# A two-layer model in fp32: feed-forward layers with one single chunk and five pairs of seven products, T3 summed by VectorE

## The reference

```python
D_MODEL = 1024
D_FF = int(math.ceil(8 * D_MODEL / 3 / 256) * 256)      # 2816

def swiglu(x, w_gate, w_up, w_down):
    return (jax.nn.silu(x @ w_gate) * (x @ w_up)) @ w_down

for i in range(DEPTH):                                  # DEPTH = 2
    ...
    u = rms_norm(h, ffn_norm_g[i])
    h = h + swiglu(u, ffn_w_gate[i], ffn_w_up[i], ffn_w_down[i])
    gate = jax.nn.sigmoid(rms_norm(h, ple_norm_g[i]) @ ple_w_gate[i])
    h = h + gate * (p[i] @ ple_w_proj[i])
```

## Time and profile before

| what | value |
|---|---|
| median of 3 runs (lowest to highest) | 1003.75 us (1002.15 to 1005.62) |
| the profiled execution: time | 1003.63 us |
| the profiled execution: span | 1001.6 us |
| PE, TensorE matmul, busy | 988.1 us, 99% |
| DVE, VectorE, busy | 775.3 us, 77% |
| ACT, ScalarE, busy | 609.2 us, 61% |
| POOL, GpSimd, busy | 153.6 us, 15% |
| DMA | 242.01 MB, 242 GB/s on average |

### The profile page before, as it was taken

The page is one execution under the profiler, slowest core; times in us unless marked ns, Lnnn a source line. Parts: engine busy times, 40 slices in busy tenths (PEclk is TensorE's granted clock), DMA queues, the critical chain, the costliest instruction groups (busy, mean ns, idle before and its releaser), DMA issues.

```text
span 1001.6 us, 13597 instructions
## 1 busy us (share of the span) xinstructions
PE 988.1 (99%) x5350; PEld 835.5 (83%) x5350; DVE 775.3 (77%) x909; ACT 609.2 (61%) x722; POOL 153.6 (15%) x150
## 2 busy tenths in 40 slices
PE   8999999999999999999999999999999999999997
PEld 8977888888778888788888888788888889999886
DVE  6996888879567666787988857876877788777874
ACT  6437567657376668666676646754857574444733
POOL 4992101101030320111111002100100010000000
PEclk9999999999999999999999999999999999999999
DMA  8862899999784632779999864577789898545631
GB/s 324 256 217 90 274 298 324 334 300 305 209 292 161 238 128 85 256 264 300 331 343 338 256 218 167 189 256 280 262 258 341 237 311 299 186 169 179 220 126 43
DMA packets 37726, 242.01 MB, mean 242 GB/s; under 512 B 4504, under 2 KB 7064, under 8 KB 9760
## 3 DMA queue, kind: packets, MB, share of 16 engines
q1 hardware_dynamic: 23904, 167.26, 43.8%
q0 software_dynamic: 10736, 70.71, 28.2%
q10 hardware_dynamic: 3024, 3.18, 1.3%
HBM read 237.91 MB, written 3.21 MB: 241 GB/s over the span
## 4 chain that ended last, share of the span: by engine, by line
PE 80%; DVE 8%; DMA 6%; issue 3%; ACT 1%; POOL 0%; SPq 0%; ACTq 0%; POOLq 0%; DVEq 0%
PE bank L441 45%; PE bank L564 18%; DVE bank L2160 4%; PE bank L427 4%; PE bank L429 4%; PE bank L428 4%; DMA raw<-in_ws 4%; DMA arena<-in_ws 3%; PE bank L478 2%; DVE w_lo L1857 2%; PE bank L603 1%; PE bank L847 0%; DMA u_scr<-arena 0%; PE bank L944 0%; PE bank L977 0%
## 5 line engine op out<-in xcount | busy, mean ns | idle before, releaser
L1857 DVE TENSOR_TENSOR w_lo<-raw,w_hi 128x2048 fp32r<-128x2048 f32 x145 | 332.8, 2303 | 84.0 <-ACT w_hi L1297 83.7
L1297 ACT ACTIVATE w_hi<-raw 128x2048 fp32r<-128x2048 f32 x156 | 298.2, 1912 | 107.9 <-PE bank L441 71.3
L1297 ACT ACTIVATE w_hi<-arena 128x2048 fp32r<-128x2048 f32 x48 | 92.4, 1924 | 57.2 <-PE bank L441 21.0
L441 PE MATMUL bank<-w_hi,x_hi 128*128 128x512 f32 x416 | 115.0, 398 | 0.2
L1857 DVE TENSOR_TENSOR w_lo<-arena,w_hi 128x2048 fp32r<-128x2048 f32 x48 | 109.2, 2285 | 5.3 <-ACT w_hi L1297 5.2
L441 PE MATMUL bank<-w_lo,x_hi 128*128 128x512 f32 x416 | 111.5, 390 | 0.0
L441 PE MATMUL bank<-w_hi,x_lo 128*128 128x512 f32 x416 | 111.5, 390 | 0.0
L441 PE MATMUL bank<-w_hi,z_hi 128*128 128x512 f32 x320 | 94.2, 394 | 0.3 <-DVE z_lo L1972 0.3
L441 PE MATMUL bank<-w_lo,z_hi 128*128 128x512 f32 x320 | 92.9, 390 | 0.1
L441 PE MATMUL bank<-w_hi,z_lo 128*128 128x512 f32 x320 | 92.9, 390 | 0.0
L441 PEld LDWEIGHTS bank<-w_hi,x_lo 128*128 128x128 f32 x416 | 78.1, 188 | 16.8
(11 more groups left out here) (292 smaller groups left out, 1592.3 us busy)
## 6 DMA issues: line engine op xcount, KB each, us to landing
raw<-in_ws SPq DMA_DIRECT2D x156, 1024.0 KB, 7.3
arena<-in_ws POOLq DMA_DIRECT2D x60, 1024.0 KB, 11.4
arena<-u_scr ACTq DMA_DIRECT2D x16, 142.0 KB, 4.9
arena<-in_rows POOLq DMA_DIRECT2D x2, 1024.0 KB, 6.6
toep<-bias_row POOLq DMA_DIRECT2D x1, 1536.0 KB, 44.7
h<-in_x_tok SPq DMA_DIRECT2D x2, 512.0 KB, 4.0
raw<-in_ws SPq DMA_DIRECT2D x2, 512.0 KB, 8.0
arena<-in_rows POOLq DMA_DIRECT2D x2, 512.0 KB, 7.5
```

What stands on the lines that cost most here:

```text
L441: ins = pe.matmul(dst, tok(a_part, k, t), w_part[:, s, c], start=first and j == 0 and i == 0, stop=last and j == 2 and i == len(ks) - 1)
L1297: act.activation(w_hi[:, g % SPLIT, :], operand(g), ACT.Copy).then_inc(hi_done, 1)
L1857: dve.tensor_tensor(w_lo[:, g % SPLIT, :], operand(g), w_hi[:, g % SPLIT, :].bitcast(F32), ALU.subtract).then_inc(lo_done, 1)
```

## The change

Chunk 0 stays single. The pairs are now (1,2), (3,4), (5,6), (7,8) and (9,10), so each layer has five pairs instead of four and one single chunk instead of three. Within the first and the last pair there is one down, within the others two, and the downs 7, 10 and 9 come last. B21's product p2 now stands second in a pair, behind B11's. T3's accumulating DMA on GpSimd's queue is gone: VectorE adds B21 to T2 in place, behind T2's low part, and SyncE's reload of B21's slot waits for that. The banks of a pair alternate between (2, 1, 0) and (1, 2, 0) for (b1, b4, b2). The first T2 is summed behind chunk 0's last quarter.

```diff
-STEPS = (0, 1, (2, 3), (4, 5), (6, 7), (8, 9), 10)
+STEPS = (0, (1, 2), (3, 4), (5, 6), (7, 8), (9, 10))
...
+WITHIN = {(1, 2): (0,), (3, 4): (2, 1), (5, 6): (4, 3), (7, 8): (6, 5), (9, 10): (8,)}
+BEHIND = (7, 10, 9)
+
+TURNED = {(1, 2): (0,), (3, 4): (2, 1), (5, 6): (4, 3), (7, 8): (6, 5), (9, 10): (8, 7)}
...
+FFN_ORDER = [("gu", 0, 0), ("gu", 0, 1)]
+for _p in PAIRS:
+    FFN_ORDER += [(_p, "B11"), (_p, "B21"), (_p, "T1"), (_p, "T2"), (_p, "B22"), ("down", WITHIN[_p][0]), (_p, "T4")]
+    FFN_ORDER += [("down", i) for i in WITHIN[_p][1:]] + [(_p, "T3")]
+FFN_ORDER += [("down", i) for i in BEHIND]
...
+                            if old == ffn_at(layer, p, "B21"):
+                                sum_there(sp, layer, p, "T3")
...
                 def pair(p):
 
                     one, two = p
                     n = pair_no(layer, p)
-                    b1, b4, b2 = [(1 + PAIRS.index(p) + j) % 3 for j in range(3)]
+                    b1, b4, b2 = ((2, 1, 0), (1, 2, 0))[PAIRS.index(p) % 2]
                     turned, within = TURNED[p], WITHIN[p]
                     product(("p1", n), ffn_at(layer, p, "B11"), *of_x(0, t0), b1, True, (S("c_11"), 2 * n - 1))
                     hidden_job(turned[0])
-                    if n == NPAIR * layer + 1:
+                    product(("p2", n), ffn_at(layer, p, "B21"), *of_x(1, t0), b2, True, (S("c_11"), 2 * n))
+                    if p == PAIRS[0]:
                         pe.wait_ge(S("q_lo"), layer + 1)
                     product(("p5", n), ffn_at(layer, p, "T1"), *of_q(0), b4, True, (S("c_22"), 2 * n - 1))
                     product(("p6", n), ffn_at(layer, p, "T2"), *of_q(1), b1, False, (S("c_12"), 2 * n - 1))
-                    if turned[1] is not None:
-                        hidden_job(turned[1])
+                    for i in turned[1:]:
+                        hidden_job(i)
                     product(("p3", n), ffn_at(layer, p, "B22"), *of_q(2), b4, False, (S("c_12"), 2 * n))
                     down(within[0])
-                    product(("p2", n), ffn_at(layer, p, "B21"), *of_x(1, t0), b2, True, (S("c_11"), 2 * n))
                     product(("p7", n), ffn_at(layer, p, "T4"), *of_q(3), b1, False, (S("c_22"), 2 * n))
-                    down(within[1])
+                    for i in within[1:]:
+                        down(i)
                     product(("p4", n), ffn_at(layer, p, "T3"), *of_x(1, t1), b1, False, (S("hidden"), MADE_NO[layer, one, 1]))
...
-            def third_sum(layer, p):
-
-                lo_ready(pool, ffn_at(layer, p, "T2"))
-                pool.dma_start(sums[:, 1, :], ws[PIECE_OF[ffn_at(layer, p, "B21")]], accum_op=ALU.add) \
-                    .then_inc(S("t3_in"), 16)
-
...
+                def third_sum(p):
+
+                    lo_ready(dve, ffn_at(layer, p, "T2"))
+                    o = ffn_at(layer, p, "B21")
+                    loaded(dve, PIECE_OF[o])
+                    dve.tensor_tensor(sums[:, 1, :], sums[:, 1, :], operand(o), ALU.add).then_inc(S("t3"), 1)
...
                     hidden_lo(turned[0])
                     ahead(o + 1)
+                    p_2, _ = take(dve, ("p2", n))
+                    dve.wait_ge(S("c_11"), 2 * n - 1)
+                    dve.tensor_tensor(c_11, p_2[:, :], c_11, ALU.add).then_inc(S("c_11"), 1)
                     ahead(o + 2)
-                    if turned[1] is not None:
-                        hidden_lo(turned[1])
+                    dve.wait_ge(S("c_11"), 2 * n)
+                    gated(one, 0, c_11[:, 256:512])
+                    third_sum(p)
+                    for i in turned[1:]:
+                        hidden_lo(i)
+                    ahead(o + 3)
```

162 lines of the change are left out of this document (56 added, 106 removed).

## The result

The changed kernel takes 1039.58 us, median of 5 runs (1038.95 to 1039.96), against 1003.75 (of 5 runs too, 1002.15 to 1005.62): a ratio of 1.0351, 95% interval 1.0336 to 1.0366. It is slower, as forecast, but by 35.8 us and not by 23, just above the range of 1013 to 1037. The profiled execution spans 1037.9 us.

The account below looks back on a forecast made before the run. TensorE was taken to set the end, with VectorE's fixed order making it wait. 1003.63 + 12.7 for the second layer + 10.4 for the first = 1026.7, so 1027 us, range 1013 to 1037.

Parts of the forecast that it names:

- TensorE's work: One pair more per layer takes away 12 matmuls, 2.7 us a layer; PE busy time falls by about 5 us.
- A middle pair: 33.0 us instead of 30.9; VectorE idles for p7 until TensorE leaves T4's product, and for a high part's late-freed slot.
- The cover I named: Missing T3 sum (2.2 us) and p2's combination and quarter behind the first down had hidden the wait; worth 3.2 together.
- The first pair: Waits at chunk 0's transposes 2.1, B22's bank 0.55, the down 2.3 and last T3 0.9: together 5.85 us.
- T1's transfers: VectorE's T2 sum waits for T1's load and accumulation: taken as 0, at most 2.2 us in each layer's first border.
- The second layer: 15.45 us of waiting over five pairs, less 2.7 saved by TensorE: +12.7 us.
- The first layer: Same 173.3 us stretch as the second layer, against 162.9 before: +10.4 us, if its idle gaps go.
- its idle gaps: First layer's gaps before its last downs, taken as waits for raw pieces that VectorE's slower pace removes; 0 to 2.4 us uncertain.
- the transfers at 0: Cost of the changed DMA issues per layer: nothing, and 0 to -2 us in the first layer.
- VectorE didn't keep up: Rival that VectorE's order leaves no wait in the pairs: 996 us, or 998 if the gaps stay; chance 0.08.
- the fixed waits: Rival that only waits not from VectorE's backlog remain, 4.45 us per layer: 1004.7 us, no change; chance 0.05.
- no T1 was late: Rival that each T1 transfer comes 2 us too late at all eight pair borders: 1043 us; chance 0.12.

Follow-up runs that it names:

- e9: Changed kernel with B21's product fifth in all five pairs, VectorE's T2 sum in its old place and the bias row's spreading issued at 75 us; 1028.18 us.
- g1: Changed kernel with B21's product second only in the first pair, fifth in the other four, and VectorE's T2 sum ahead of the next B11's low part; 1021.83 us.
- e10: Changed kernel with the T3 sum left out altogether, done by neither VectorE nor GpSimd, and no SyncE wait for it; 1022.64 us.
- e6: Changed kernel with only the bias row's spreading issued earlier by GpSimd, at 75 us; 1033.74 us.
- g3: Changed kernel with VectorE's T3 sum adding another resident tensor of the same size, so SyncE's reload doesn't wait for it; 1030.48 us.
- g2_mended: Against g1, two VectorE steps moved: chunk 0's second quarter ahead of B21's low part, first pair's T3 sum behind B22's combination; 1018.06 us.
- e3: Kernel before, with four pairs and B21's product in its old place, but T3 summed by VectorE instead of GpSimd's transfers; 1011.48 us.

## Why the prediction was right and wrong

- **TensorE's work, -2.7 us a layer:** right by the count of matmuls (5326 against 5350) and by periods of 30.9 us in five pairs (e9, g1). That its busy time would fall by 5 us was wrong, it rose by 4.0.
- **A middle pair, 33.0 us:** right, 33.2. VectorE is busy 29.0 us as counted, and idle at the two places named. The waits are 0.65 before T1's product (0.6 counted) and 1.12 at the down's low part (1.5 counted); the rows show 1.8 of the 2.3 us. The cover I named is confirmed from both sides: without the sum 32.1, with B21 back in its place 30.9. I had put its worth at 3.2 us together and didn't see that B21's place, with the T2 sum's place and the banks that went with it, holds all of it. These three weren't taken apart. With B21 second, T1's product takes the bank that T3 has just left, so it waits for the last quarter; with B21 fifth it has the third bank. The Trainium skill (Perfetto Trace Analysis, Optimization Strategy) says that a gap that repeats can mean too few buffers for the next tile; the 0.65 us, which e10 didn't remove, agree.
- **The first pair, 5.85 us:** rows show 1.69, 0.51, 1.99 and 0.87, together 5.1 (2.1, 0.55, 2.3 and 0.9 counted). Second pair 1.8 against 2.4, last pair 2.6 against 3.0, each with some 0.3 us per wait that no row shows.
- **T1's transfers, 0:** right; no T2 sum waited for a DMA.
- **The second layer, +12.7:** +14.0. The term of the middle pairs was 0.2 us short in each.
- **The first layer, +10.4, "if its idle gaps go":** it measured +21.8, and this is the miss. The gaps weren't the cause. The first layer of before was 2.4 us longer than the second; in e6 and g3 the first layer's tail is within 0.3 us of the second's, so they did go. After the change the first layer is 10.2 us longer than the second, all of it in the tail (50.7 against 40.5): 14.0 - 2.4 + 10.2 = 21.8. The step that failed is a cost put at nothing. I had the transfers at 0, in the first layer at 0 to -2 us, and the change's new wait of SyncE for the T3 sum has no term and no reason for having none. I never asked what the held reload meets when it is late. It meets the spreading of the bias row: issued 18 us later than before (251.4 against 233.3), behind five pairs instead of four, beside pieces that three downs in a row need soon. That is 7.3 us of wait and, by difference, 2.6 of a slower clock: g3, without the hold, has 9.9 us less tail. With these 9.9 us my own terms would have given 1037; the rest is the 1.3 us that each layer's pairs cost more than counted.
- **The rivals:** VectorE didn't keep up, the fixed waits weren't all, and no T1 was late. That the clock would bring the time above my range if it fell behind a gap was written down, but for gaps of 2 us; it fell behind the one of 7.3.

No version beats the kernel before: the best, g2_mended, is 1.5% slower (1.1 to 1.8). Five adjacent pairs save 2.7 us a layer, yet g2's second layer is 7.5 us longer than before's; 6.3 us of waits stand in its rows (1.3, 0.5, 1.1, 0.9 and 2.5). The first three, 2.9 us, are in the first pair, whose start, as I read it, the second single chunk had covered.

## What to carry over

When a step is moved onto a busy engine, its place in the order decides, not its length: the same 2.2 us cost nothing behind T4's low part with B21 fifth (e9), 0.8 us a pair one low part later (e3, four pairs), and 1.1 us a pair with B21 second (e10). When an engine's step becomes a condition for a reload, look at what that reload will travel beside when it starts later, once for each copy of the loop, since the copies differ in their neighbours. And a slow transfer on a shared queue has no free place until all that stands behind it has been read off.
